# From gated sums to expert queries in one block, with sums and features in pairs of chunks

## The reference

```python
merged = jax.nn.sigmoid(gate_a) * (oa @ w_up_a[l]) + jax.nn.sigmoid(gate_b) * (ob @ w_up_b[l])
y = (merged @ w_o[l]) * gt1[:, None]
x = layer_norm(DN_ALPHA * x + y, ln_g[l, 0], ln_b[l, 0])

hf = x * (1.0 + sc2[:, None]) + sh2[:, None]
y = peer_ffn(hf, w_pq[l], sub_keys[l], peer_u[l], peer_v[l]) * gt2[:, None]
x = layer_norm(DN_ALPHA * x + y, ln_g[l, 1], ln_b[l, 1])
```

## Time and profile before

| | |
|---|---|
| median of 3 runs | 4042.52 us (4018.96 to 4042.55) |
| the profiled execution | 4049.3 us, its span 4047.4 us |
| PE busy | 2703.8 us, 67% |
| DVE busy | 2649.2 us, 65% |
| ACT busy | 995.0 us, 25% |
| HBM | 255 GB/s over the span |

### The profile page before, as it was taken

The page is one execution under the profiler, slowest core; times in us unless marked ns, Lnnn a source line. Parts: engine busy times, 40 slices in busy tenths (PEclk is TensorE's granted clock), DMA queues, the critical chain, the costliest instruction groups (busy, mean ns, idle before and its releaser), DMA issues. The chain is left out here.

```text
span 4047.4 us, 44570 instructions
## 1 busy us (share of the span) xinstructions
PE 2703.8 (67%) x16804; PEld 2346.9 (58%) x16804; DVE 2649.2 (65%) x3875; ACT 995.0 (25%) x1395; POOL 959.0 (24%) x1028
## 2 busy tenths in 40 slices
PE   6867648948389407776749930000399999996899
PEld 5647427847178406565428830000399899994599
DVE  3624586676777795635686679999755655556454
ACT  2233211010110003232210010000254555543354
POOL 0000015455454460000024447666200000000000
PEclk8978769979699758877769965555699999998699
DMA  6543479999899993533579999999555455550153
GB/s 236 190 165 137 174 286 406 412 386 413 313 387 412 377 360 135 188 125 114 234 286 405 412 350 404 380 379 387 197 169 180 156 174 171 173 176 21 52 169 133
DMA packets 229391, 1034.48 MB, mean 256 GB/s; under 512 B 29672, under 2 KB 32632, under 8 KB 180088
## 3 DMA queue, kind: packets, MB, share of 16 engines
q0 software_dynamic: 147456, 536.94, 34.0%
q1 hardware_dynamic: 81784, 495.51, 33.6%
HBM read 1031.30 MB, written 1.05 MB: 255 GB/s over the span
## 5 line engine op out<-in xcount | busy, mean ns | idle before, releaser
L272 DVE TENSOR_TENSOR w_lo<-raw,w_hi 128x1024 fp32r<-128x1024 f32 (+1 forms) x492 | 557.7, 1138 | 602.1 <-ACT w_hi L259 602.0
L1768 POOL DMA_INDIRECT arena_layer<-in_peer_u,arena_layer x512 | 479.6, 937 | 1576.2 <-SPq L861 1167.1
L1820 DVE CUSTOM_DVE_ANT_0 arena_layer<-arena_layer,ps 128x1024 f32<-128x1024 f32 x512 | 612.7, 1220 | 183.3 <-DMA arena_layer<-in_peer_u,arena_layer 171.5
L1816 DVE SCALAR_TENSOR_TENSOR ps<-arena_layer,ps 128x1024 f32<-128x1024 f32 x512 | 660.3, 1290 | 79.5 <-DMA arena_layer<-in_peer_v,arena_layer 54.2
L650 PE MATMUL ps<-hT_hi,w_hi 128*128 128x256 f32 x2240 | 642.8, 287 | 45.2 <-PEq L791 25.1
L259 ACT ACTIVATE w_hi<-raw 128x1024 fp32r<-128x1024 f32 (+1 forms) x492 | 485.0, 989 | 705.1 <-PE ps L650 703.7
L650 PE MATMUL ps<-hT_lo,w_hi 128*128 128x256 f32 x2240 | 641.1, 286 | 0.0
L650 PE MATMUL ps<-hT_hi,w_lo 128*128 128x256 f32 x2240 | 640.9, 286 | 0.0
L650 PE MATMUL ps<-parts_context,raw 128*128 128x256 f32 x2496 | 549.8, 384 | 58.6 <-PEq L861 58.6
L1768 POOL DMA_INDIRECT arena_layer<-in_peer_v,arena_layer x512 | 479.1, 936 | 331.2 <-DVE ps L1816 313.1
L650 PEld LDWEIGHTS ps<-parts_context,raw 128*128 128x128 f32 x2496 | 482.3, 193 | 125.8 <-issue 59.8
(11 more groups left out here) (339 smaller groups left out, 2959.3 us busy)
## 6 DMA issues: line engine op xcount, KB each, us to landing
raw<-in_ffn_w_gu SPq DMA_DIRECT2D x154, 1024.0 KB
raw<-in_w_mod SPq DMA_DIRECT2D x72, 1024.0 KB
raw<-in_w_ada SPq DMA_DIRECT2D x48, 1024.0 KB
raw<-in_w_in SPq DMA_DIRECT2D x44, 1024.0 KB
raw<-in_ffn_w_down SPq DMA_DIRECT2D x56, 768.0 KB
raw<-in_ffn_w_down SPq DMA_DIRECT2D x56, 640.0 KB
raw<-in_conv_w_in SPq DMA_DIRECT2D x24, 1024.0 KB
raw<-in_w_o SPq DMA_DIRECT2D x8, 1024.0 KB
```

The source lines that it names most:

```text
L272: dve.tensor_tensor(self.lo[:, k, 0:n], self.raw_part(g, parity, k // 2, g.starts(k), g.starts(k + 1)), self.hi[:, k, 0:n].bitcast(F32), A ...
L1768: gp.indirect_dma_start(self.grow[:, slot % GR, :], None, self.tables[slot // half_way], bass.IndirectOffsetOnAxis(ap=self.index[:, k:k + ...
L1816: dve.scalar_tensor_tensor(out=self.tile, in0=row, scalar=cell, in1=self.tile, op0=ALU.mult, op1=ALU.add) \
L1820: dve.tensor_tensor_reduce(row, row, self.tile, 1.0, 0.0, ALU.mult, ALU.add, cell).then_inc(row_used.sem, 1)
```

## The change

All three functions now register their code in one block, so that the engines meet once behind `peer_queries`, and semaphores order what the meetings ordered before.

- `merge`: the gate row's broadcast moves to its start (from that of `output_projection`), with its copy to `rows` on ACT; tile two's product is multiplied, added, rounded and split in four pairs of chunks; the split of the last quarter of `w_o`'s first tile comes between two pairs on DVE. PE's `ready(pair)` waits for a pair's split.
- `output_projection`: the residual of the first 512 columns is made when `w_o`'s first tile is done, beside the second. The root's table is loaded early. Only the normalised tokens (`normed`, kept in `y_tok`) go to PE; gain and shift of the norm are folded into the columns `scol` and `bcol` with which ACT modulates (`full`), so `x_tok` gets gain and shift afterwards, behind the splits. The features are turned, modulated and split in pairs.
- `peer_queries`: `hf_tok` comes from `y_tok` with the folded rows; the keys' load has its own semaphore.
- The setup loads `ln_g` and `ln_b` as rows to be turned into columns.

```diff
+            small(vrows[V_LNG:V_LNG + 32, 1, :], a["ln_g"].rearrange("l k (r p) -> (l k r) p", p=P))
+            small(vrows[V_LNB:V_LNB + 32, 2, :], a["ln_b"].rearrange("l k (r p) -> (l k r) p", p=P))
...
+    def merge(block, l, oaT, obT, gates):
...
+        @block.tensor
+        def _(pe):
+            broadcast_row(pe, lambda c: adacol[:, l, 16 + c:17 + c], 2).then_inc(gate_row_made.sem, 1)
+            for k, src in enumerate((oaT, obT)):
+                if k:
+
+                    pe.wait_ge(gate_row_kept.sem, gate_row_kept.at(1))
+                project_features(pe, k, lambda b, k=k: ps[:, 2 * k + b // 4,
+                                                          b % 4 * SEQ:(b % 4 + 1) * SEQ], src)
...
+            split_ahead(dve=dve, tile=(1, 1, 0), quarters=range(HI_EARLY))
+            product_wait(dve, 1)
+            for pair in range(KC // 2):
+                at = slice(2 * pair, 2 * pair + 2)
+                src = ps[:, 2 + pair // 2, pair % 2 * 512:(pair % 2 + 1) * 512]
+                v.link(dve.tensor_tensor(other[:, at, :], other[:, at, :],
+                                         src.rearrange("p (b t) -> p b t", t=SEQ), ALU.mult))
+                dve.tensor_tensor(own[:, at, :], own[:, at, :], other[:, at, :], ALU.add) \
+                   .then_inc(merged.sem, 1)
+                if pair:
+                    split(pair - 1)
+                if pair == 2:
+                    split_ahead(dve=dve, tile=(1, 1, 0), quarters=range(HI_EARLY, QUARTERS))
+            split(KC // 2 - 1)
...
+    def output_projection(block, l, ready, scale, shift, full):
...
+        @block.tensor
+        def _(pe):
+            for t in range(2):
+                project_tokens(pe, t, tiles_of(t), hT, arrive=None if t else ready)
+
+            def turn(t, c):
+                at = c % 4 * SEQ + t * P
+                return pe.transpose(ps[:, 2 + c // 4, at:at + P],
+                                    normed[:, t, c * P:(c + 1) * P], ident[:])
+
+            pe.wait_ge(x_normed.sem, x_normed.at(1))
+            for c in range(KC):
+                turn(0, c)
+            for pair in range(KC // 2):
+                if pair % 2 == 0:
+                    pe.wait_ge(x_normed.sem, x_normed.at(2 + pair // 2))
+                for c in (2 * pair, 2 * pair + 1):
+                    mm = turn(1, c)
+                mm.then_inc(pair_turned.sem, 1)
...
+            product_wait(dve, 0)
+            for t in range(TT):
+                residual(t, 0)
+            split_ahead(dve=dve, tile=(1, 1, 0), quarters=range(LO_EARLY))
+            product_wait(dve, 1)
+            for t in range(TT):
+                residual(t, 1)
+                v.wait()
+                dve.bn_aggr(stat[:, 2 * t:2 * t + 2], stat[:, 16 + 12 * t:28 + 12 * t]) \
+                   .then_inc(ln_variance.sem, 1)
...
+            for pair in range(KC // 2):
+                dve.wait_ge(pair_modulated.sem, pair_modulated.at(pair + 1))
+                at = slice(2 * pair, 2 * pair + 2)
+                v.link(dve.tensor_copy(hT_hi[:, at, :], full[:, at, :]))
+                dve.tensor_tensor(hT_lo[:, at, :], full[:, at, :], hT_hi[:, at, :].bitcast(F32),
+                                  ALU.subtract).then_inc(pair_split.sem, 1)
+            split_ahead(dve=dve, tile=(1, 1, 0), quarters=range(LO_EARLY, QUARTERS))
+
+            dve.wait_ge(loaded.sem, loaded.at(32))
+            dve.wait_ge(x_normed.sem, x_normed.at(3))
+            for t in range(TT):
+                v.link(dve.tensor_tensor(x_tok[:, t, :], normed[:, t, :], rows[:, 1, :], ALU.mult))
+                dve.tensor_tensor(x_tok[:, t, :], x_tok[:, t, :], rows[:, 2, :], ALU.add) \
+                   .then_inc(x_renewed.sem, 1)
```

More of the change, by code:

```diff
@@ L360, in _build @@
     eps = sb("eps", [P, 1])
+    ln_eps = sb("ln_eps", [P, 1])
     rows = sb("rows", [P, 3, D])
@@ L435, in _build @@
     hidden_made = signal("hidden_made")
+    merged = signal("merged")
+    merged_rounded = signal("merged_rounded")
+    merged_split = signal("merged_split")
+    ln_variance = signal("ln_variance_made")
+    ln_rooted = signal("ln_rooted")
+    x_renewed = signal("x_renewed")
+    keys_loaded = signal("keys_loaded")
     conv_gated = signal("conv_gated")
@@ L537, in _build @@
     V_NG, V_CW = 16, 112
+    V_LNG, V_LNB = 80, 72
     with nc.Block(no_gpsimd_drain=True) as block:
@@ L1316, in stick_breaking @@
         pe_done.base += 3 * groups
[L1318 to L1348, removed]
-                dve.tensor_tensor(gates[:, 0:KC, :], gates[:, 0:KC, :], gates[:, KC:2 * KC, :],
-                                  ALU.add).then_inc(vec_ready.sem, 1)
-                dve.wait_ge(act_ready.sem, act_ready.at(1))
-                v.tick(dve.tensor_tensor(hT_lo[:], gates[:, 0:KC, :], hT_hi[:].bitcast(F32),
-                                         ALU.subtract))
-        vec_ready.base += 1
-        act_ready.base += 1
-        weights.end()
     def residual_norm(dve, act_, v, pieces, gate, gain, shift):
@@ L2972, in _build @@
         gate_projection(l, gates)
-        merge(l, oaT, obT, gates)
-        output_projection(l)
         hf_tok, index, gate, small, rest = carve((TT, D), (TT, PEER_HEADS, TOPK),
                                                  (TT, PEER_HEADS, TOPK), (128,), (8576,))
-        modulated_features(x_tok, adacol[:, l, 32:40], lambda c: adacol[:, l, 24 + c:25 + c],
-                           rest[:, 0:2048].rearrange("p (c t) -> p c t", t=SEQ))
         index = index.bitcast(U32)
@@ L2993, in _build @@
         eq = rest[:, 2048:4096].rearrange("p (h n) -> p h n", h=PEER_HEADS)
-        peer_queries(l, hf_tok, pqT, keys, keysT, sc)
+        with nc.Block(no_gpsimd_drain=True) as block:
+            ready = merge(block, l, oaT, obT, gates)
+            arrive = output_projection(block, l, ready, adacol[:, l, 32:40], adacol[:, l, 24:32],
+                                       rest[:, 0:2048].rearrange("p (c t) -> p c t", t=SEQ))
+            peer_queries(block, l, hf_tok, pqT, keys, keysT, sc, arrive)
         peer_select(l, sc, best, bestf, cand, pos, p12, eq, sel, index, gate)
```

259 lines of the change are left out of this document (166 added, 93 removed).

## The result

The changed kernel takes 3988.02 us (median of 4 runs, 3985.87 to 3994.4), the one before 4042.53 (4 runs, 4018.96 to 4046.18): a ratio of 0.9881, 95% interval 0.9845 to 0.9917. Predicted were 3987.7 us and a gain of 54.8; measured is 54.5. The ratio is an estimate of its own over the undisturbed (fast) runs, and not the quotient of the two medians: by it the gain is 48 us, and 34 to 63 with its interval. The profiled execution went from a span of 4047.4 to one of 3984.1 us. That the sum came out to a third of a microsecond is luck: the interval is far wider than that, and terms of the sum were off in opposite directions, as the stages show.

The account below looks back on a forecast made before the run. Bound taken: a chain where PE and DVE take turns, no engine full. Terms 11.4 - 1.8 + 18.1 + 0.1 = 27.8 us a layer, 55.6 for both, less 0.8: 54.8 off 4042.52 gives 3987.7; range 3957 to 4006.

Parts of the forecast that it names:

- Merge pause: Between `w_up_b`'s last matmul and `w_o`'s first product: PE's gap falls from 14.9 to 3.5 us, 11.4 won a layer.
- Norm pause: Between `w_o`'s last matmul and `w_pq`'s first: the gap falls from 28.9 to 10.8 us a layer.
- the 18.1: Microseconds won a layer behind `w_o`, said to contain gain and shift, two block ends, wide modulation and wide split.
- Head of `merge`: Gate row's broadcast, unhidden ahead of `w_up_a`, partly replaces slow-clock time: 1.8 us lost a layer, 3.4 at the other end.
- Clock: Half-clock stretches at the heads of `w_o` and `w_pq`: 3.4 us lost before, 3.3 after, 0.1 won, 1.5 either side.
- The rule on transposes: Transposes don't count as PE work, so `w_pq`'s head stays slow: 0.8 us worse a layer, 3989.
- Setup and jumps: Two small setup loads lose 0.8 us once; jumps between functions, hidden by DVE, cost nothing, 2 us at most.
- The covers: Rival: DVE runs late and PE waits at quarters in both halves, 13 us lost, 4001; chance 0.10.
- given back: Rival: the stretch behind waits for its own transfers, undoing the gain: 4042, or 4015 with half lost; chance 0.07.
- The gathers' waits: Rival: DVE's waits for gathered rows in the expert groups grow, by 42% for 4083; slower, chance 0.03.
- The kernel's two speeds: Rival: the changed kernel runs like the faster earlier run of 4018.96, giving 3964; chance 0.10.
- three outcomes below 4002: The forecast itself (0.70), covers failing (0.10) and the faster speed (0.10), together called faster.

Follow-up runs that it names:

- The late residual: Changed kernel with the residual of the first 512 columns made behind `w_o`'s second tile, as before the change: 3980.48 us, ratio 0.9824.
- the repeat: The changed kernel run again without any edit, on a chip with longer and scattered times: 4078.24 us, ratio 0.989.
- the broadcast in the pause: Changed kernel with the gate row's broadcast moved from the head of `merge` into PE's 3.5 us pause behind `w_up_b`: 3971.99 us, ratio 0.9822.

## Why the prediction was right

- **Merge pause.** 3.5 predicted, 3.52 measured in both layers. The linked and unlinked durations held, and so did the cover of the later pairs. That pairs in their own block win only 1.8 us was not in the prediction; there the two effects are one sum.
- **Norm pause.** 10.8 predicted, 10.45 measured. PE turns 5.61 us after `w_o` (6.0 predicted), and the rest is the 4.8 us of the earlier trace rows, although that row's turning takes 3.12 and this one 3.67. What the 18.1 is said to contain leaves out the split that stood ahead of the residual (2.2 by the timelines). The late residual (4.1) and the folding (2.9) are each shown by their own undoing.
- **Head of `merge`.** The term "1.8 lost" was mis-sized, and is no constant: -0.3 in layer 0 (the broadcast at 2.02, full clock) and +1.3 in layer 1 (3.03). In the repeat it is +1.3 in both. The broadcast sits where the clock is slow, so it takes the place of part of the slow time, as argued, and by more than I took. That the whole place was avoidable, the broadcast in the pause shows: 1.6 to 1.8 back against the repeat, and 0.1 against the layer where the clock was full.
- **Clock.** The term "0.1 won" was mis-sized. Predicted was 3.3 us of half clock at `w_o`; it is 5.2 us at 0.50 in layer 1 and at 0.67 in layer 0, so `w_o` is 0.6 and 1.6 longer than before. `w_pq`, at 0.52 for 4.6 us, is as slow as before (25.2 against 25.4), where I had taken 0.75 off. Together the term is some 0.4 to 1.5 lost a layer instead of 0.1 won, 1.9 in both layers; on the mean within the 1.5 to either side, in layer 1 at its edge. The norm pause (0.35 a layer better) and the head (1.3 a layer better on the mean) make up for it, by luck.
- **The rule on transposes** of the Trainium skill ("TensorE: Matmul & The Clock Gate", Part 4) gave a slow head of `w_pq`, and slow it was, by the 0.52. But its reason did not hold here: 28 transposes in the pause kept the clock full up to the product just as matmuls did, and in the kernel with the broadcast in the pause the clock rose while PE did nothing but transposes, so that `w_pq` starts at 1.00. The number came out, the cause did not.
- **Setup and jumps.** No run shows the term "0.8 lost": PE's first matmul of the modulation behind the setup starts at 16.93 (17.00 before), and `merge` of layer 0 starts at 332.5 to 336.2 in the eleven profiles with the new setup, at 334.6 before. Nor do the jumps show in either pause.
- **Rivals.** The covers held. Nothing was given back behind the chain. The gathers' waits did not grow. The kernel's two speeds show again (4018.96 and 4042.5 before, and 4018.76 and 4019.62 among nine later runs), but none of the changed kernel's four runs lies near 3964; what makes them is still open. The chances of the three outcomes below 4002 add up to 0.90, where the prediction has 0.89.

## What to carry to other kernels

A step cut into pieces pays only where the consumer can start on the first piece, so cut the step and remove the barrier behind it together: 8.0 us here, against 1.8 and nothing for each alone. When a pause of TensorE has become short, move its own small work (broadcasts, transposes) from exposed places into the pause: it hides, and TensorE comes out of the pause at full clock, which was worth 2.5 us behind pause 1 and 3.0 behind pause 2. Read edits of a few microseconds from the lengths of stages in the trace; whole times of one kernel spread here by 8 to 42 us in four runs, and by 49 in ten. And count a gain of clock only if it repeats in layers and kernels: the 2.3 us behind `w_pq` came and went with no edit to it.

## What the runs showed of the hardware

- Pauses that end on DVE's chain repeat to 0.02 us over runs and chips (3.52 to 3.53 in nine profiles with pairs in one block, both layers), while PE stages behind them vary by up to 2.6 us with the granted clock: `w_o` took 22.05 to 24.61 behind the same bare pause of 3.52 us.
- The clock at a start of PE depends on more than the idle time before it. Behind a turning after the same 5.61 us of idle, `w_pq`'s head was granted 0.52 in one kernel and 1.00 in another; and behind the same pause, `w_o`'s head had 0.67 in one layer and 0.50 in the other layer of one run. Whether earlier activity decides, or the moment at which the pause falls, is open.
- Work of TensorE whose result is discarded kept the clock from falling in a pause and made two stages shorter, by 3.0 us a layer together; transposes and matmuls did it alike. The clock also rose from 0.50 to 1.00 while TensorE did nothing but transposes (16 of them, behind 5.61 us of idle).
- The end of a block costs 0.4 to 0.54 us beyond the last engine's work. Its real price is that last engine's work.
